# A gated-attention layer on one core: the gate's 16 columns made beside the key's instead of in two steps of their own

## The reference, cut to what matters

```python
h = rmsnorm(x, norm_mix_pre) @ w_in     # columns: q 256, k 256, v 512, g 512, a 16, u 512, sv 512
loga = log_sigmoid(a @ w_gate_up + b_gate) / 16      # a: (1024, 16) -> (1024, 256)
cum = cumsum(loga within each chunk of 64 positions)
k_dec = k * exp(cum[end of chunk] - cum)
state = exp(cum[end of chunk]) * state + k_dec^T v    # chunk after chunk
o = (q * 64**-0.5) @ state of the own chunk
```

## Time and profile before

| | |
|---|---|
| median of 3 executions | 1336.89 us (1334.82 to 1337.28) |
| the profiled execution | 1333.69 us, of which its span is 1331.7 us |
| PE busy | 1286.8 us, 97% of the span |
| DVE, ACT, POOL busy | 734.6, 543.1, 217.4 us |
| mean granted PE clock | 0.994 of full speed |

### The profile page before, as it was taken

One profiled execution on the slowest core, in us unless ns is written; L12 is line 12 of the kernel. 1 busy time (PEld: TensorE's weight loads), 2 busy tenths in 40 slices (PEclk: granted clock), 3 DMA queues, 4 the chain that ended last, 5 costly groups with the idle time before them and its releaser, 6 DMA issues.

```text
span 1331.7 us, 17011 instructions
## 1 busy us (share of the span) xinstructions
PE 1286.8 (97%) x6409; PEld 1079.5 (81%) x6409; DVE 734.6 (55%) x1111; ACT 543.1 (41%) x1022; POOL 217.4 (16%) x340
## 2 busy tenths in 40 slices
PE   6989999999999999999988999999999999999996
PEld 6988898778888888888867888888888887888885
DVE  4664331346433564454597666766666655555645
ACT  5876142432222453344454333333333333445431
POOL 2222000111000220002100000001555445000012
PEclk9999999999999999999998999999999999999998
DMA  6768111111133111112124555555455457797723
GB/s 238 264 227 293 50 63 48 33 38 49 58 112 110 33 48 48 64 42 86 48 80 151 189 200 195 192 188 188 153 179 178 157 196 249 226 365 233 228 86 118
DMA packets 74193, 189.71 MB, mean 142 GB/s; under 512 B 9280, under 2 KB 9856, under 8 KB 72704
## 3 DMA queue, kind: packets, MB, share of 16 engines
q1 hardware_dynamic: 62544, 151.35, 33.8%
q0 software_dynamic: 11520, 37.27, 7.5%
q10 hardware_dynamic: 48, 0.01, 0.0%
HBM read 137.22 MB, written 51.38 MB: 142 GB/s over the span
## 4 chain that ended last, share of the span: by engine, by line
PE 89%; DVE 4%; ACT 2%; DMA 2%; issue 2%; POOL 1%; DVEq 0%; SPq 0%; ACTq 0%; POOLq 0%
PE ps L1561 28%; PE ps L1563 28%; PE ps L1562 28%; PE ps L1586 2%; DMA tok<-in_x 1%; DVE w_lo L510 1%; ACT ps L826 1%; PE ps L1660 1%; DMA wsT<-in_b_spatial 0%; POOL rstd L730 0%; PE ps L1634 0%; DMA score_weights<-stage_a 0%; DVE sums_lo L1368 0%; ACT w_hi L501 0%; DVE state L1333 0%
## 5 line engine op out<-in xcount | busy, mean ns | idle before, releaser
L1561 PE MATMUL ps<-w_hi,act_hi 128*128 128x512 f32 (+1 forms) x704 | 273.4, 388 | 0.0
L1563 PE MATMUL ps<-w_hi,act_lo 128*128 128x512 f32 (+1 forms) x704 | 267.8, 380 | 0.0
L1562 PE MATMUL ps<-w_lo,act_hi 128*128 128x512 f32 (+1 forms) x704 | 267.4, 380 | 0.0
L1563 PEld LDWEIGHTS ps<-w_hi,act_lo 128*128 128x128 f32 x704 | 132.4, 188 | 25.4
L1561 PEld LDWEIGHTS ps<-w_hi,act_hi 128*128 128x128 f32 x704 | 132.5, 188 | 25.2 <-issue 1.5
L1562 PEld LDWEIGHTS ps<-w_lo,act_hi 128*128 128x128 f32 x704 | 132.6, 188 | 23.7
L1562 PE MATMUL ps<-act_lo,w_hi 128*128 128x512 f32 x384 | 150.5, 392 | 0.0
L1343 DVE TENSOR_TENSOR w_lo<-wraw,w_hi 128x512 fp32r<-128x512 f32 x132 | 98.3, 747 | 91.6 <-ACT w_hi L962 91.6
L1561 PE MATMUL ps<-sums_hi,w_hi 128*128 128x512 f32 x352 | 138.5, 394 | 6.0 <-ACT spare L1000 4.0
L1563 PE MATMUL ps<-sums_hi,w_lo 128*128 128x512 f32 x352 | 138.0, 392 | 0.0
L1349 DVE TENSOR_TENSOR w_lo<-wraw,w_hi 128x1024 fp32r<-128x1024 f32 x66 | 83.1, 1263 | 79.2 <-ACT w_hi L973 78.9
(11 more groups left out here) (238 smaller groups left out, 2160.5 us busy)
## 6 DMA issues: line engine op xcount, KB each, us to landing
wraw<-in_w_ffn_gu SPq DMA_DIRECT2D x44, 512.0 KB, 4.1
ffn<-in_w_ffn_down SPq DMA_DIRECT2D x22, 512.0 KB, 4.3
hidden_a<-ffn POOLq DMA_DIRECT2D x44, 256.0 KB, 3.4
down_sums<-ffn SPq DMA_DIRECT2D x11, 1024.0 KB, 3.8
hidden_s<-ffn POOLq DMA_DIRECT2D x44, 256.0 KB, 2.4
wraw<-down_sums SPq DMA_DIRECT2D x44, 256.0 KB, 4.5
wraw<-hidden_s SPq DMA_DIRECT2D x44, 256.0 KB, 3.5
raw<-in_w_in SPq DMA_DIRECT2D x20, 512.0 KB, 3.5
```

The source lines that it names most:

```text
L1561: nc.tensor.matmul(out_, lh, rh, start=first, stop=False, skip_group_check=onto)
L1562: nc.tensor.matmul(out_, lh, rl, start=False, stop=False, skip_group_check=onto)
L1563: return nc.tensor.matmul(out_, ll, rh, start=False, stop=last, skip_group_check=onto)
```

## The change

- The two a steps are gone, with `wa`, its clearing by POOL and POOL's wait for the nine stores. STEPS has 140 entries.
- The q steps take the second 128 query columns first. Once both their steps are done, DVE writes the split gate columns over the last 16 query columns in `w_hi` and `w_lo`, which lie just ahead of the key columns.
- A k step is 272 columns wide: 16 of the gate and 256 of the key. ACT copies the 16 columns first, into `a_rows` (two buffers), then the key.
- One step later PE turns them (`turn_gate`, 128 x 16 to 16 x 128), and DVE copies them to `aT` (`gate_rows`). Two steps later come the gate's second product and the five instructions behind it (`gate`), on every engine. So the gates of tiles 6 and 7 now fall in the v steps 0 and 1.
- The second product has 33 rows instead of 65.

The diff (indentation reduced; left out: the names of semaphores, "a" struck from `chunk_of` and `freed_by`, and the condition of an activation-table load of ACT, now behind the last q step):

```diff
@@ -129,7 +129,7 @@
 if name in ("xk", "xv"):
     STEPS += [(name, b, f) for f in range(4)]
 elif name == "qk":
-    STEPS += [("q", 0, f) for f in range(4)] + [("a", 0, f) for f in range(2)]
+    STEPS += [("q", 0, f) for f in range(4)]
     STEPS += [("k", 0, t) for t in range(TT)]
 elif (name, b) == ("o", 0):
@@ -263,12 +263,14 @@
 stage = place("stage", [P, 3, CW], F32, at["gain"])
 stage_a = [place(f"stage_a{i}", [P, CW], F32, at["act_lo"] + (4 * i + 2) * K) for i in range(3)]
 stage_b = place("stage_b", [P, 3, CW], F32, at["half"] + 8 * K)
-wa = place("wa", [P, KT, CHUNK], F32R, at["spare"])
+
+wa_hi, wa_lo = (w[:, CNO[("qk", 0)] % 2, :, KW - RANK:KW] for w in (w_hi, w_lo))
 wsT = little("wsT", [P, HEADS, P])
 ident = little("ident", [P, P])
 later = little("later", [P, P])
 inchunk = little("inchunk", [P, 2])
 wg = little("wg", [P, KW])
+a_rows = little("a_rows", [P, 2, RANK])
 decay = little("decay", [P, TT, 4])
 VECTORS = [("mem", norm_mem, KT), ("mix", norm_mix_pre, KT), ("x", norm_x_pre, KT),
@@ -360,6 +362,9 @@
 def o_psum(rows, h):
     return ps[rows, (O, TR)[h % 2], (h // 2) * DV:(h // 2 + 1) * DV]
+def a_psum(t):
+    return ps[0:RANK, (TR + 1, U)[t % 2], 0:P]
+
 def z_psum(t):
     return ps[:, (Z, O)[t % 2], 0:KW]
@@ -741,7 +747,7 @@
     rstd_of(("mem", 0))
     rstd_of(("mem", 1))
-    for r, src in ((0, w_gate_up[0]), (32, w_gate_up[0]), (CHUNK, b_gate[0:1, :])):
+    for r, src in ((0, w_gate_up[0]), (32, b_gate[0:1, :])):
         pool.dma_start(wg[r:r + src.shape[0], :], src).then_inc(small_landed, 16)
     at_step = {SNO["xo" if n >= 16 else "xq", n % 16 // 8, n % 8]: n for n in range(32)}
     for n in range(len(STEPS)):
@@ -750,13 +756,9 @@
         if n in at_step:
             store(at_step[n])
-    for no in range(9):
-        pool.wait_ge(stored[no], 16 * stage_uses(no, 32))
-    pool.memset(wa[:, :, :].bitcast(F32), 0.0).then_inc(consts, 1)
-
-    pool.wait_ge(consts, 5)
     pool.wait_ge(tr_done, TRNO["x", 7] + 1)
-    pool.memset(aT[CHUNK:CHUNK + 1, :], 1.0).then_inc(consts, 1)
+    pool.memset(aT[0:32, :], 0.0).then_inc(consts, 1)
+    pool.memset(aT[32:33, :], 1.0).then_inc(consts, 1)
     pool.wait_ge(consts, 6)
     pool.memset(state[:, 1, 1, :, :], 0.0).then_inc(consts, 1)
     pool.wait_ge(consts, 7)
@@ -872,6 +874,13 @@
         slot_free(act, p)
         splits_hi(act, split_parts(p))
+    def gate(t):
+        act.wait_ge(z_read, t + 1)
+        zt = resid[:, t, 0:KW]
+        nc.scalar.activation(zt, zt, ACT.Exp).then_inc(gate_e, 1)
+        act.wait_ge(gate_e, t + 1)
+        nc.scalar.activation(zt, zt, ACT.Ln, bias=1.0).then_inc(gate_l, 1)
+
     def evac(n):
         kind, b, t = STEPS[n]
         if kind in ("xk", "xv"):
@@ -888,14 +897,16 @@
             nc.scalar.activation(stage_of(m), bank(n), ACT.Copy).then_inc(free_act, 1)
         elif kind == "k":
             act.wait_ge(mm_done, n + 1)
-            nc.scalar.activation(resid[:, t, CW:CW + KW], bank(n, KW), ACT.Copy).then_inc(free_act, 1)
-
-            act.wait_ge(z_read, t + 1)
-            zt = resid[:, t, 0:KW]
-            nc.scalar.activation(zt, zt, ACT.Exp).then_inc(gate_e, 1)
-            act.wait_ge(gate_e, t + 1)
-            nc.scalar.activation(zt, zt, ACT.Ln, bias=1.0).then_inc(gate_l, 1)
+            if t >= 2:
+                act.wait_ge(a_turned, t - 1)
+            nc.scalar.activation(a_rows[:, t % 2, :], bank(n, RANK), ACT.Copy).then_inc(a_read, 1)
+            nc.scalar.activation(resid[:, t, CW:CW + KW], bank(n)[:, RANK:RANK + KW],
+                                 ACT.Copy).then_inc(free_act, 1)
+            if t >= 2:
+                gate(t - 2)
         elif kind == "v":
+            if t < 2:
+                gate(TT - 2 + t)
             act.wait_ge(suf_done, t + 1)
             nc.scalar.activation(resid[:, t, KW:2 * KW], ps[:, SUF, 0:KW], ACT.Exp,
@@ -1203,6 +1214,21 @@
         ins.then_inc(resid_ready, 1)
         dve.wait_ge(resid_ready, t + 1 + (TT if kind == "o" else 0))
+    def gate_rows(t):
+        dve.wait_ge(a_turned, t + 1)
+        if t == 0:
+            dve.wait_ge(consts, 6)
+        nc.vector.tensor_copy(aT[0:RANK, t * P:(t + 1) * P], a_psum(t)).then_inc(a_ready, 1)
+
+    def gate(t):
+        dve.wait_ge(z_done, t + 1)
+        zm, za = resid[:, t, KW:2 * KW], resid[:, t, 0:KW]
+        link(nc.vector.tensor_scalar(zm, z_psum(t), 0.0, None, ALU.min))
+        nc.vector.scalar_tensor_tensor(out=za, in0=zm, scalar=2.0, in1=z_psum(t),
+                                       op0=ALU.mult, op1=ALU.subtract).then_inc(z_read, 1)
+        dve.wait_ge(gate_l, t + 1)
+        nc.vector.tensor_tensor(za, zm, za, ALU.subtract).then_inc(loga_ready, 1)
+
     def evac(n):
         kind, b, t = STEPS[n]
         if kind in ("xk", "xv"):
@@ -1212,27 +1238,22 @@
                                     ALU.subtract).then_inc(free_dve, 1)
         elif kind == "q":
-            pair, hf = divmod(t, 2)
+            pair, hf = 1 - t // 2, t % 2
             dve.wait_ge(mm_done, n + 1)
             o = CW + KW + pair * P
             nc.vector.tensor_scalar(resid[:, 4 * hf:4 * hf + 4, o:o + P],
                                     bank(n).rearrange("p (t n) -> p t n", t=4), DK ** -0.5, None,
                                     ALU.mult).then_inc(free_dve, 1)
-        elif kind == "a":
-            dve.wait_ge(mm_done, n + 1)
-            nc.vector.tensor_copy(aT[0:CHUNK, t * CW:(t + 1) * CW], bank(n)[0:CHUNK, :]).then_inc(free_dve, 1)
         elif kind == "k":
-
-
-            dve.wait_ge(z_done, t + 1)
-            zm, za = resid[:, t, KW:2 * KW], resid[:, t, 0:KW]
-            link(nc.vector.tensor_scalar(zm, z_psum(t), 0.0, None, ALU.min))
-            nc.vector.scalar_tensor_tensor(out=za, in0=zm, scalar=2.0, in1=z_psum(t),
-                                           op0=ALU.mult, op1=ALU.subtract).then_inc(z_read, 1)
-            dve.wait_ge(gate_l, t + 1)
-            nc.vector.tensor_tensor(resid[:, t, 0:KW], resid[:, t, KW:2 * KW], resid[:, t, 0:KW],
-                                    ALU.subtract).then_inc(loga_ready, 1)
+            if t:
+                gate_rows(t - 1)
+            if t >= 2:
+                gate(t - 2)
         elif kind == "v":
+            if t == 0:
+                gate_rows(TT - 1)
+            if t < 2:
+                gate(TT - 2 + t)
             dve.wait_ge(suf_read, t + 1)
             dve.wait_ge(free_act, free_count(SNO["k", 0, t], "act"))
             kk = resid[:, t, CW:CW + KW]
@@ -1462,17 +1483,18 @@
         if STEPS[n] == ("xo", 1, 7):
             dve.wait_ge(part_landed, 32)
-            dve.wait_ge(small_landed, 16 * 3)
-            dve.wait_ge(consts, 5)
             for k in range(KT):
                 ins = nc.vector.tensor_scalar(raw_a[:, k, :], raw_a[:, k, :], pre["mix"][:, k:k + 1],
                                               None, ALU.mult)
                 ins.then_inc(dve_own, 1)
             own[0] += KT
-            dve.wait_ge(dve_own, own[0])
-            link(nc.vector.tensor_copy(wa[:, :, 0:RANK], raw_a[:, :, :]))
-            nc.vector.tensor_tensor(wa[:, :, 32:32 + RANK], raw_a[:, :, :],
-                                    wa[:, :, 0:RANK].bitcast(F32), ALU.subtract).then_inc(wa_ready, 1)
+            a_scaled = own[0]
+        if STEPS[n] == ("q", 0, 2):
+            dve.wait_ge(dve_own, a_scaled)
+            dve.wait_ge(mm_done, SNO["q", 0, 1] + 1)
+            link(nc.vector.tensor_copy(wa_hi, raw_a[:, :, :]))
+            nc.vector.tensor_tensor(wa_lo, raw_a[:, :, :], wa_hi.bitcast(F32),
+                                    ALU.subtract).then_inc(wa_ready, 1)
         if then:
             then()
         for kind, t in TR_AT[n]:
@@ -1600,6 +1622,20 @@
                 transposes(("xn3", 6))
         ins.then_inc(mm_done, 1)
+    def turn_gate(t):
+        pe.wait_ge(a_read, t + 1)
+        nc.tensor.transpose(a_psum(t), a_rows[:, t % 2, :], ident[:, :]).then_inc(a_turned, 1)
+
+    def gate(t):
+        if t == 0:
+            pe.wait_ge(small_landed, 16 * 2)
+            pe.wait_ge(consts, 7)
+        elif t >= 2:
+            pe.wait_ge(z_read, t - 1)
+        pe.wait_ge(a_ready, t + 1)
+        nc.tensor.matmul(z_psum(t), aT[0:33, t * P:(t + 1) * P], wg[0:33, :],
+                         start=True, stop=True).then_inc(z_done, 1)
+
     pe.wait_ge(consts, 1)
     pe.wait_ge(rows_landed, 16 * 3)
     pe.wait_ge(rows_landed_pool, 16 * (len(VECTORS) - 3))
@@ -1699,8 +1735,9 @@
                             (w_hi[:, s, k, :], w_lo[:, s, k, :]), f == 0, f == 1)
             ins.then_inc(mm_done, 1)
         elif kind == "q":
-            pair, hf = divmod(t, 2)
-            if hf == 0 and pair == 0:
+
+            pair, hf = 1 - t // 2, t % 2
+            if t == 0:
                 pe.wait_ge(tr_lo, 2 * (TRNO["x", 7] + 1))
             for k in range(KT):
                 if t == 0 and k % 2 == 0:
@@ -1709,31 +1746,24 @@
                 ins = three(bank(n), (w_hi[:, s, k, qs], w_lo[:, s, k, qs]),
```

(36 more changed lines are left out.)

## The result

| | before | after |
|---|---|---|
| median | 1336.92 us (5 executions, 1334.82 to 1337.28) | 1343.76 us (5, 1342.61 to 1344.45) |
| the profiled execution | 1333.69 us, span 1331.7 | 1342.61 us, span 1340.9 |

The ratio of after to before is 1.0054, with a 95% interval of 1.0039 to 1.0068: 6.8 us slower. 1341.6 us had been forecast for the median, with a range of 1333.5 to 1346. The profiled execution before was 3.2 us under its median, the one after only 1.2, so the two profiles lie 8.9 us apart and not 6.8.

The account below looks back on a forecast made before the run. PE was taken to bound the kernel, busy 97% of the span. Terms -7.4 + 1.3 + 0.9 + 5.0 + 2.1 + 2.8 = +4.7 us took the median from 1336.9 to 1341.6 us; range 1333.5 to 1346.

Parts of the forecast that it names:

- the two waits: PE standing ahead of the suffix sums of v1 and v2, 5.0 us, and before the network's first product, 2.1 us.
- a steps gone: Removing the two a steps, which filled PE from 149.76 to 157.12, saves 7.36 us, all on the path.
- Wider products: In the k steps, 8 x 24 products become 16 columns wider at 0.42 ns a column, adding 1.3 us.
- Turns: Eight PE transposes of the gate's 16 columns, 0.109 us each, add 0.9 us.
- The gate product, costed at nothing: The gate's second product, one per tile, was taken at 0.44 us as before, with nothing added for its changed rows.
- The gate's waits: At v0 and v1 ACT does the gate before reading the suffix sums, so PE waits 2.5 us twice, 5.0 us.
- The bank: With 140 steps the last uses bank 1, so the network's first product starts 3.0 us late, 2.1 us net.
- The clock: Two of the three new PE gaps lower the granted clock to half, at 1.4 us each, adding 2.8 us.
- that only one wait shows: Rival, chance 0.17: either the gate's waits or the bank's are hidden; 1333.8 to 1335.2 us or 1336.7 to 1339.5.
- that none shows: Rival, chance 0.10: neither the gate's waits nor the bank's appear, giving -5.2 us, 1331.7 us, faster.
- That the clock holds: Rival, chance 0.10: both waits appear but PE keeps its full clock; +1.9 us, 1338.8 us.
- That 272 columns stream like plain float32: Rival, chance 0.03: the k steps' wider products run at plain float32 price, 192 of them adding over 60 us.

Follow-up runs that it names:

- E5: E4 with the gate's second product over 65 rows again, 32 of them zero, instead of 33; 1330.16 us, ratio to before 0.9950.
- E1: The changed kernel with ACT reading the suffix sums before the gate of tile 6 or 7 at v0 and v1; 1334.33 us, ratio to before 0.9988.
- E2: The changed kernel with every step's PSUM bank shifted so the last step lands in bank 0, as before; 1342.31 us, ratio to before 1.0049.
- E3: The kernel before, with only the steps' PSUM banks shifted by one so its last step lands in bank 1; 1337.93 us, ratio 1.0012.
- E4: The changed kernel with the edits of E1 and E2 together; 1332.29 us, ratio to before 0.9971.
- E6: E4 with the turn moved behind slice 3 of the step's product, still 33 rows; 1330.97 us, ratio to before 0.9958.
- E7: E5 with E6's edit, so 65 rows and the turn in the middle of the step's product; 1329.44 us, ratio to before 0.9942.

## Why the prediction was right

The direction, the two waits and their places came as forecast; 4.7 us had been forecast and 6.8 measured, inside the range. Of the signs that it named, three came otherwise: a k step took 3.89 us and not 3.6, its products 0.123 each and not 0.127, and the profile put the waits ahead of the suffix sums down to DVE and not to ACT's second reading. By its own terms:

- **a steps gone**, 7.4: as forecast. No run takes them away by themselves; the sum of stage a, k below closes with it.
- **Wider products**, 1.3 forecast. 48 products of 272 columns take 157.54 - 151.62 = 5.92 us, 0.1233 each, 0.0037 more than 256 columns instead of 0.0067. 192 of them cost 0.7. So 16 columns more cost 0.23 ns a column between 256 and 272, and 0.42 between 256 and 512. The text gave 256 columns bound by the weight load, with nothing to pay, as its lower end; the truth lies in the middle, and what bounds a product of 256 columns wasn't tested.
- **Turns**, 0.9 forecast. Alone, one costs 157.78 - 157.54 - 0.12 = 0.12, eight 1.0. The 275 ns by the page of the Trainium skill, TensorE: Matmul & The Clock Gate (PE-mode transpose), agree with how long a turn itself lasts in the timeline, 0.27 us; but that is no cost in a stream of products, and the 2.2 us worked out from it isn't what was measured.
- **The gate product, costed at nothing**, is the step that failed. "The second product has 33 rows instead of 65" was described and not priced. It cost 0.38 a time, 3.0 us for eight (E5). Stages a and k gained 4.5 us, where these terms without it give: 7.4 - 0.7 - 0.8 for seven turns + 0.9 for the two gate products that moved on = 6.8; less 6 times 0.38, 4.5.
- **The gate's waits**, 5.0 forecast. From the turn PE went on after 3.20 us instead of 3.05, but turn and gate product took 0.83 of that themselves instead of 0.55, so each gap lost about 2.4: 4.7 for both. E1 shows the cause.
- **The bank**, 2.1 forecast, 2.1 measured (E2), in all its parts: a gap of 2.91, and no wait left at the third product, where 0.76 stood before. The transposes of the last tile start 695.61 - 687.36 = 8.25 after the first product, and 685.14 - 675.91 = 9.23 before. The gap of 4 us moved as a whole.
- **The clock**, 2.8 forecast as two of three at 1.4. In the profile two of three it was, but an estimated 1.7 and 3.1, since behind the second gap the half clock was granted for 6.83 us and not 3.41. Stage v holds some 4.5 of it (E1), the network's gap none here and 1.6 in E1 and E3. Gaps as long as these keep the clock in some executions (E3), so that just two of three lost it is in part luck.

The terms, as measured: -7.4 + 0.7 + 1.0 + 3.0 + 4.7 + 2.1 + 4.5 = +8.6 for the profiled execution, which is what the three stages lost together. The clock's 4.5 is what E1 leaves once the gaps are taken off, so this sum isn't a proof of it. The median lost 6.8. Executions differ in how much clock their gaps cost, front and rest vary by more than that difference, and the profiled execution before was faster than all five that its median is taken from, so it isn't settled further. That the total came nearer than its terms is in part luck: 3.0 for the rows was forgotten and the clock was 1.7 too low, while the wider products were 0.6 too dear, and the median lost 1.8 less than the three stages of the profile.

Of the rivals, that only one wait shows and that none shows are out (E1, E2). That the clock holds is out for this profile and for E2's, which has the same two gaps in stage v and the half clock behind both. That 272 columns stream like plain float32 is out: 0.123 each.

## What to carry to other kernels

When work is put off by a step or two, look where the tail of it lands: ACT and DVE are strict lists, and an item that waits for PE must stand behind every item that PE waits for. When the number of steps changes, work out anew which buffer the last one gets; a rotation by step number couples the start of the next stage to it, hundreds of microseconds away. And price each operand whose row count changes, even to a smaller one: here 33 rows were dearer than 65.

## What the runs showed of the hardware

- The weight load of a plain float32 stationary operand of 33 rows isn't hidden beside the product ahead, where that has 128 rows: it starts only with its own product, and the next load of 128 rows starts only with the product behind. That costs 0.38 us more than with 65 rows, 32 of them zeros put in for it (E4, E5, E6, E7). The kernel before had rows that hinted at it. At its first chunk product of g, with operands of 64 rows, the load starts with the product too, behind an idle time of 0.35, put down to issue:

```profile
234.48 0.44 PEld L1648 LDWEIGHTS ps<-half,resid 64*64 64x64 f32 x16 [0.35 <-issue]
234.48 0.68 PE L1648 MATMUL ps<-half,resid 64*64 64x128 f32 x16
```

  The same 0.35 stands ahead of the load at all nine places of that trace where products of 64 rows follow products of 128, and ahead of none of its sixteen loads of 65 rows is there any. Those products of 64 rows differ in other things too, so whether the limit lies between 64 and 65 rows, and what in the array sets it, wasn't tried.
- A granted clock of 0.50 followed gaps of 2.3 us before PE's next instruction twice in the profile after and twice in E2's; it followed one of 2.91 us in E1 and E3 and not in the changed kernel. The length of a gap alone doesn't tell. An older gap, ahead of the first product of L1561 with `kv_hi` (L1583 in the changed kernel), shows the same. In the kernel before it is 2.17 us long and the full clock holds; in the changed kernel it is shorter, 2.02, and the half clock follows it (the timeline's row of the product, then the stretch behind it, for either kernel):

```profile
59.38 0.36 PE L1561 MATMUL ps<-kv_hi,w_hi 128*128 128x256 f32 x1 [2.17 <-DVE kv_lo L1211]
59.40:62.80 3.40, 3.40 (x29) 3.40 (x30) 1.03 (x2) 1.72 (x3) 0.59 (x1) 1.00 0.75 272
```

```profile
59.87 0.36 PE L1583 MATMUL ps<-kv_hi,w_hi 128*128 128x256 f32 x1 [2.02 <-DVE kv_lo L1237]
61.14:64.55 3.41, 3.41 (x19) 3.41 (x18) 0.92 (x2) 1.82 (x3) 0.63 (x1) 0.50 0.47 176
```

  The products of 256 columns bear the clock out: they start 0.12 us apart in the first stretch and 0.21 in the second.
